# A decoder block in split fp32: the first projection stage with all sixteen k tiles split into high and low parts, and new orders behind it

## What is computed

```python
mod = silu_c @ w_ada[l] + b_ada[l]
sh1, sc1, g1, sh2, sc2, g2 = jnp.split(mod, 6, axis=-1)
h = modulate(rms_norm(x, norm1_w[l]), sh1, sc1)
proj = h @ w_in[l]
...
mixed = jnp.concatenate([y_ret, y_dif], axis=-1).astype(x.dtype) @ w_out[l]
x = x + g1[:, None, :] * mixed
h2 = modulate(rms_norm(x, norm2_w[l]), sh2, sc2)
mlp = jnp.square(jax.nn.relu(h2 @ w_mlp1[l])) @ w_mlp2[l]
x = x + g2[:, None, :] * mlp
return rms_norm(x, final_norm_w)
```

## Time and profile before

| | us |
|---|---|
| median of 3 runs | 2373.59 |
| lowest, highest | 2372.52, 2373.86 |
| profiled execution, its own time | 2372.57 |
| its span | 2370.7 |
| PE busy | 2312.1 (98%) |
| DVE busy | 1264.7 (53%) |
| ACT busy | 754.5 (32%) |

### The profile page before, as it was taken

One profiled execution on the slowest core, in us unless ns is written; L12 is line 12 of the kernel. 1 busy time (PEld: TensorE's weight loads), 2 busy tenths in 40 slices (PEclk: granted clock), 3 DMA queues, 4 the chain that ended last, 5 costly groups with the idle time before them and its releaser, 6 DMA issues.

```text
span 2370.7 us, 28575 instructions
## 1 busy us (share of the span) xinstructions
PE 2312.1 (98%) x10384; PEld 1883.6 (79%) x10384; DVE 1264.7 (53%) x1801; ACT 754.5 (32%) x1025; POOL 77.5 (3%) x59
## 2 busy tenths in 40 slices
PE   4999999999999999999999999999999999999998
PEld 2568888878787788888888888888888888888887
DVE  7977988866666675733333333333333333333354
ACT  3233343344545422421221221221221322222233
POOL 0011110100101000000000000000000000000000
PEclk9999999999999999999999999999999999999999
DMA  9956677622222574232222222222222222222222
GB/s 377 402 205 218 228 269 248 247 95 84 73 87 70 189 274 168 80 107 97 97 93 95 96 97 97 97 97 97 97 94 94 94 97 97 97 97 96 99 89 98
DMA packets 90630, 328.25 MB, mean 138 GB/s; under 512 B 10064, under 2 KB 10576, under 8 KB 89936
## 3 DMA queue, kind: packets, MB, share of 16 engines
q1 hardware_dynamic: 89568, 326.41, 39.3%
q10 hardware_dynamic: 1008, 1.13, 0.1%
HBM read 323.31 MB, written 4.19 MB: 138 GB/s over the span
## 4 chain that ended last, share of the span: by engine, by line
PE 87%; DVE 9%; ACT 2%; issue 1%; DMA 1%; POOL 0%; SPq 0%; POOLq 0%; ACTq 0%; DVEq 0%
PE bank L437 27%; PE bank L438 27%; PE bank L441 27%; DVE ada_sb L1058 3%; DVE w_lo L1051 2%; PE bank L578 1%; DVE prob L1058 1%; PE bank L544 1%; PE bank L461 1%; DMA xy<-x_t 1%; PE bank L569 0%; PE bank L492 0%; DMA prob<-ada 0%; ACT w_hi L757 0%; ACT L850 0%
## 5 line engine op out<-in xcount | busy, mean ns | idle before, releaser
L437 PE MATMUL bank<-act_hi,w_hi 128*128 128x512 f32 (+1 forms) x2112 | 828.8, 393 | 13.1 <-DVE act_lo L1098 4.6
L438 PE MATMUL bank<-act_lo,w_hi 128*128 128x512 f32 (+1 forms) x2112 | 819.9, 389 | 0.0
L757 ACT ACTIVATE w_hi<-raw 128x1024 fp32r<-128x1024 f32 x392 | 413.8, 1056 | 896.0 <-PE bank L441 841.5
L1051 DVE TENSOR_TENSOR w_lo<-raw,w_hi 128x1024 fp32r<-128x1024 f32 x392 | 491.9, 1257 | 308.9 <-ACT w_hi L757 296.0
L441 PE MATMUL bank<-act_hi,w_lo 128*128 128x512 f32 (+1 forms) x2112 | 518.3, 387 | 0.0
L437 PEld LDWEIGHTS bank<-act_hi,w_hi 128*128 128x128 f32 x2112 | 397.8, 188 | 101.5 <-issue 17.7
L438 PEld LDWEIGHTS bank<-act_lo,w_hi 128*128 128x128 f32 x2112 | 397.7, 188 | 81.9 <-issue 1.7
L441 PEld LDWEIGHTS bank<-act_hi,w_lo 128*128 128x128 f32 x2112 | 394.5, 188 | 81.1
L437 PE MATMUL bank<-u_hi,w_hi 128*128 128x512 f32 (+1 forms) x1040 | 401.6, 387 | 0.0
L438 PE MATMUL bank<-u_lo,w_hi 128*128 128x512 f32 (+1 forms) x1040 | 400.2, 386 | 0.0
L1453 DVE SCALAR_TENSOR_TENSOR xy<-bank,modr,xy 128x512 f32 (+1 forms) x141 | 105.9, 751 | 413.2 <-PE bank L441 413.2
(11 more groups left out here) (152 smaller groups left out, 1121.7 us busy)
## 6 DMA issues: line engine op xcount, KB each, us to landing
raw<-weights SPq DMA_DIRECT2D x400, 512.0 KB, 3.2
ada_sb<-ada SPq DMA_DIRECT2D x172, 512.0 KB, 5.4
prob<-ada SPq DMA_DIRECT2D x20, 512.0 KB, 6.7
xy<-x_t SPq DMA_DIRECT2D x16, 512.0 KB, 6.1
out<-rows_out SPq DMA_DIRECT2D x4, 1024.0 KB, 4.8
decay_sb<-decay SPq DMA_DIRECT2D x7, 256.0 KB, 3.1
silu_c<-c_row SPq DMA_DIRECT2D x1, 1024.0 KB, 5.6
rot_sb<-rot ACTq DMA_DIRECT2D x2, 256.0 KB, 7.1
```

Of the source, the lines that this page charges most:

```text
L437: pe.matmul(acc, stationary, hi, start=first, stop=False)
L438: pe.matmul(acc, stationary, lo, start=False, stop=False)
L757: nc.scalar.activation(w_hi[:, w], raw[:, r], ACT.Copy).then_inc(hi_ready, 1)
L1051: nc.vector.tensor_tensor(w_lo[:, w], raw[:, r], w_hi[:, w].bitcast(F32), ALU.subtract).then_inc(lo_ready, 1)
```

## The change

It changes eight things:

1. WHOLE is empty: all sixteen k tiles are split; a new `first_chunk` does all eight hi x hi products first, then hi x lo, then lo x hi, and the last tile's products bank by bank, with `first_done` telling when each bank is finished.
2. DVE's dot products take a row of 2048 in one instruction and start from the bias, so that two replace four, and `modulation1` becomes one small instruction (`scale1`). The rings have the same bytes: three places of 1 MB in the first stage (NADA_1 = 3), two later.
3. c comes as one row; PE spreads it over the partitions with a vector of ones, and ACT applies SiLU in four pieces between its squares. Three of the sixteen squares are summed by PE. The squares have places of their own in `rows_out`.
4. The stages of head 0 move one chunk later (`at = j - 1`), `rotate_q` of head 0 stands ahead of `rest_w`, and the rotary and decay tables are loaded behind the first stage's chunks.
5. Table loads of ACT are written out: one table set holds both Ln and Exp, and is loaded behind the gates.
6. In the output projection and the first MLP group one tile each goes to a spare bank (4 and 6), and two waits for a bank fall away; the last head's `finish_dif` and the splits of y stand earlier.
7. The sums for the second norm take the last tile's squares on PE instead of adding them on DVE first, and the sums and the spread stand inside the half tiles.
8. At the end `last_sums` stands ahead of the last turn, and rows are scaled and stored in halves of 512 KB.

```diff
-NADA = 4
-NADA_1 = 6
+NADA = 2
+NADA_1 = 3
...
-WHOLE = tuple(range(1, KT, 2))
+WHOLE = ()
...
             for k in range(KT):
-                for a in range(4 * k, 4 * k + 4):
-                    load_ada(Count(a))
-                    if a % 4 == 2:
-                        load_raw(Count(k))
+                if k == 0:
+                    for i in range(4):
+                        load_ada_half(i)
+                else:
+                    for e in range(2):
+                        load_ada(Count(2 * k + e))
+                load_raw(Count(k))
...
+                pe.wait_ge(hi_ready, made(Count(k)))
+                pe.wait_ge(act_hi_ready, k + 1)
+                for i in range(BLOCKS):
+                    product(i, w_hi, act_hi, start=k == 0)
+                pe.wait_ge(act_ready, SPLIT.index(k) + 1)
+                if k < KT - 1:
+                    for i in range(BLOCKS):
+                        product(i, w_hi, act_lo)
+                    pe.wait_ge(lo_ready, made(Count(k)))
+                    for i in range(BLOCKS):
+                        mm = product(i, w_lo, act_hi)
+                    mm.then_inc(chunk_done, 1)
+                else:
+                    pe.wait_ge(lo_ready, made(Count(k)))
+                    for i in range(BLOCKS):
+                        product(i, w_hi, act_lo)
+                        product(i, w_lo, act_hi, stop=True).then_inc(*((first_done, 1) if i < BLOCKS - 1 else (chunk_done, 1)))
...
             def project(h, s0, slots, stage):
+                head1 = isinstance(h, int) and h == 1
                 for j in range(slots):
-                    late = j == 0 and stage is ret_stage
-                    if j in stage and not late:
-                        stage[j](h - 1)
+                    at = j - 1 if head1 else j
+                    late = at == 0 and stage is ret_stage
+                    if at in stage and not late:
+                        stage[at](h - 1)
...
             round_w(Count(FIRST))
             round_rotated(1, q_hi)
             act.wait_ge(act_ready, KT)
-            for h in range(2):
-                take_gate(h, bank[3 + h], Count(FIRST))
+            for h in range(EARLY):
+                take_gate(h, bank[3 + h], first_done, 4 + h)
+            take_gate(EARLY, bank[3 + EARLY], chunk_done, FIRST)
             round_rotated(2, k_hi)
-            for h in range(2, EARLY + 1):
-                take_gate(h, bank[3 + h], Count(FIRST))
+            load_table(LN_EXP_SET)
...
+            for k in range(KT):
+                normed(0, k)
+                if k == 0:
+                    rest_w(Count(0))
+                    modulated_rest(0, 0)
+                if k + 1 < KT:
+                    dot1(k + 1, 0)
+                if k in SPLIT and k > 0:
+                    rest_w(Count(k))
+                    modulated_rest(0, k)
+                if k + 1 < KT:
+                    dot1(k + 1, 1)
+                    scale1(k + 1)
...
-            tile_part(Count(last), 7, 0, 1, chunk_done)
-            token_sums(2)
-            tile_part(Count(last + 1), 7, 1, 1, chunk_done)
-            token_spread(2)
+            tile_part(Count(last), 7, 0, 1, chunk_done, lambda: token_sums(2))
+            tile_part(Count(last + 1), 7, 1, 1, chunk_done, lambda: token_spread(2), BLOCKS // 2)
...
+            for part in range(2):
+                for half in range(2):
+                    cols = slice(half * HALF, (half + 1) * HALF)
+                    for tb, scaled in ((2 * part, scaled_v), (2 * part + 1, scaled_s)):
+                        sp.wait_ge(scaled, 2 * part + half + 1)
+                        sp.dma_start(out[tb * P128:(tb + 1) * P128, cols], rows_out[:, tb, cols]).then_inc(out_written, 16)
```

More of the change, by code:

```diff
@@ L52 @@
 FLOOR = -3.0e38
+SPARE_OUT, SPARE_UP = 4, 6
 LN_SCALE = 2.0 ** -64
+SILU_SET, LN_EXP_SET = 18, 6
 BLOCKS = 8
@@ L451, in first_chunk, with product @@
             def first_chunk(k):
[L453 to L454 removed]
+                w = w_place(Count(k))
+                def product(i, weight, moving, start=False, stop=False):
+                    return pe.matmul(bank[i][:], weight[:, w, i * P128:(i + 1) * P128], moving[:, k], start=start, stop=stop)
+                pe.wait_ge(hi_ready, made(Count(k)))
@@ L470, in quad_chunk, with tile_part, pairs, quad_part @@
                                 for i in range(BLOCKS)], s)
-            def tile_part(s, b, half, part, done):
+            def tile_part(s, b, half, part, done, between=None, at=BLOCKS):
                 cols = half_tokens(part)
-                split_products([(i, bank[b][:, cols], act_hi[:, 8 * half + i, cols], act_lo[:, 8 * half + i, cols],
-                                 half == 0 and i == 0, half == 1 and i == BLOCKS - 1, None)
-                                for i in range(BLOCKS)], s, done)
-            def quad_part(s, j, part, between, done):
+                def pairs(blocks):
+                    return [(i, bank[b][:, cols], act_hi[:, 8 * half + i, cols], act_lo[:, 8 * half + i, cols],
+                             half == 0 and i == 0, half == 1 and i == BLOCKS - 1, None) for i in blocks]
+                w = w_place(s)
+                pe.wait_ge(hi_ready, made(s))
+                for i, acc, hi, lo, first, _, _ in pairs(range(BLOCKS)):
+                    if i == at:
+                        between()
+                    stationary = w_hi[:, w, i * P128:(i + 1) * P128]
+                    pe.matmul(acc, stationary, hi, start=first, stop=False)
+                    pe.matmul(acc, stationary, lo, start=False, stop=False)
+                if between is not None and at == BLOCKS:
+                    between()
+                pe.wait_ge(lo_ready, made(s))
+                for i, acc, hi, _, _, last, _ in pairs(range(BLOCKS)):
+                    mm = pe.matmul(acc, w_lo[:, w, i * P128:(i + 1) * P128], hi, start=False, stop=last)
+                if done is not None:
+                    mm.then_inc(done, 1)
+            def quad_part(s, j, part, between, done, early=None):
                 cols, w = half_tokens(part), w_place(s)
```

425 lines of the change are left out of this document (239 added, 186 removed).

## The result

The changed kernel takes **2359.64 us** (median of four runs, 2359.62 to 2361.32) against 2373.06 for the kernel before (2372.16 to 2373.86): a ratio of 0.9946, 95% interval 0.993 to 0.9962. The forecast was 2360.5. The profiled execution is the slowest of the four: 2361.32 us, span 2359.4, which is 11.3 less than the span before.

The account below looks back on a forecast made before the run. It took DVE to set the first stage's pace and PE to bound the kernel behind it. Terms -2.8 - 8.7 - 1.2 = -12.7 us gave 2359.9 or 2360.9, forecast 2360.5, range 2354 to 2367.

Parts of the forecast that it names:

- Start: Chain up to the first `hf`: it begins at 25.8 us where it was at 29.81; bounds no gain or 5 us.
- Pace: First stage: DVE needs 7.1 us per k tile against 6.5, with a wide dot at 2.21.
- The slower DVE that eats PE's gain: First stage: DVE gets slower by 0.6 us a tile, and the 8 us that PE saves go into waiting.
- Behind the stage: From the stage's end through the first chunks: -5.0 + 2.6 - 0.4 = -2.8 us, with no change from the clock.
- the new wait: PE behind the first chunk after the stage waits 2.6 us for the second chunk's `w_hi`; bounds 0 to 3.5.
- The first rival: Behind the stage: no wait for `w_hi` or the clock stays, -17 us, 2356.5; chance 0.18.
- Later waits: PE's waits in heads, output projection, MLP and second norm shrink: -8.7 us, bounds -5 to -10.
- merged dots in the heads save DVE time beside PE: Heads, behind the first stage: wider dots save DVE time beside PE, counted as no change in total time.
- The second rival: PE's later waits only move: two thirds coming back gives -7 us, 2366.6, all gives -4, 2369.6; chance 0.12.
- End: Last rows scaled and stored in halves, sums ahead of the last turn: -1.2 us, bounds 0 and -2.
- Ring of three: First stage: three 1 MB places are too few, DVE waits 1.1 us in some 15 tiles, 2377; chance 0.06.
- clock in every tile: First stage: PE's wait of about 1.6 us a tile brings the lower clock, +50 us, 2411; chance 0.03.

Follow-up runs that it names:

- run 3: Changed kernel with the first stage's wide dots of tiles 1 to 15 starting from constant 0.0, not the bias: 2358.89 us.
- run 4: Changed kernel with seven odd k tiles (1 to 13) whole again, every other edit kept: 2358.46 us.
- run 1: Changed kernel with the second weight chunk's high part (`w_hi`) rounded ahead of `k_hi` and the table load: 2356.62 us.
- run 5: Changed kernel with seven whole k tiles and the second weight chunk's `w_hi` rounded right behind `q_hi`: 2352.41 us.
- run 9: Changed kernel with dots of 1024 behind the first stage, their sums in a free first-stage tensor so that no tensor moves: 2357.86 us.
- run 12: Changed kernel with seven whole k tiles, the early `w_hi` and dots of 1024 in the heads with no tensor moved: 2348.96 us.
- run 2: Changed kernel with only the Ln and Exp table load moved behind the second weight chunk's `w_hi`: 2357.57 us.
- run 7: Kernel before with only the table loads written out, one set for Ln and Exp loaded behind the gates: 2369.11 us.
- run 8: Changed kernel with dots of 1024 and a sum behind the first stage, which also moved later tensors by 64 bytes: 2365.18 us.
- run 10: Changed kernel with only 64 unused bytes in a partition ahead of the later tensors: 2366.81 us.
- run 11: Changed kernel with only 128 unused bytes in a partition ahead of the later tensors: 2379.36 us.

## Why the prediction was right

Its sum, -12.7, stands against -11.25 between the two profiled executions and -13.4 between the medians of the result. That 2360.5 is only 0.9 from the median is partly luck: the terms together were 1.4 too large, and the changed kernel's median lies 1.7 below its profiled execution, where the forecast put it 1.0 above.

- **Start**: -4.0 forecast, **-6.0** measured. Squares and SiLU were priced at 0.64 each from the earlier trace rows; eight squares in a row took 4.25, 0.53 each, so DVE's sum ended at 16.89, where 18.4 was forecast. The rest of the chain, forecast a little longer, became 0.2 shorter. POOL's root fell in it from 1.85 to 1.02, which the forecast had not named: before, a dot product ran on DVE beside it, and now DVE stands idle for it (1.20). No run changes the start alone, so this term is read from the traces.
- **Pace**: 7.1 us, measured **7.20**. The dot's price was the term: 2.21 taken, 2.27 measured. All of it is the start value that comes from a tensor: without it (run 3) the dot of 102.25 has the next instruction 2.21 behind it, as forecast, and a tile takes 7.08. Over fifteen tiles the 0.1 costs 1.5. The mask and lambda cost 0.4, forecast 1.0. With the start's 2.0 that puts the last `hf` at 132.21, where the sum gives 133.3; from it to the rotation it took 4.25, forecast 3.9. Misses of opposite sign made 136.46 for 136.9, not good numbers.
- **The slower DVE that eats PE's gain**: right. The waits for `act_lo` (1.13 a tile, forecast 1.4) and 9.93 of 10 us of DVE show it, and run 4 shows the other side: with seven whole tiles the stage ends six us earlier (four to five between runs 1 and 5 and runs 9 and 12). PE was busy 6.04 us in a tile, not the 5.44 of a later chunk, so instead of two waits of 1.6 together it has one of 1.13 in most tiles; only four times does it wait for `act_hi`. The forecast said that DVE gets slower, but did not draw the conclusion that splitting fewer tiles would do more for the stage.
- **Behind the stage**: bank 0 at 136.46 (136.9), `k_hi` at 144.51 (144.8), the new wait 2.53 (2.6), the clock loss 1.7 (1.7); -3.15 at the end of head 1 against -2.8. Runs 1 and 2 show that ACT's order is the cause of the wait. The first rival (0.18) is what run 1 builds: 2356.62, where it was priced at 2356.5.
- **Later waits**: -8.7 forecast, **-7.4** measured (from -3.15 at the end of head 1 to -10.6 at the last products). What was named went: `w_hi` and L544 by the table loads (run 7: 3.0 alone, where 2.4 was claimed, 1.0 of it from y's splits), y's splits, `xy`, `issue`; the second norm gave 2.4 of its 2.7, more than the 1.7 claimed. Only the table loads were isolated by a run; for the others the lists of waits before and after are the evidence. From 150 us on PE waits 4.4 us, where 2 to 4 was forecast. The step that failed is "merged dots in the heads save DVE time beside PE", at nothing: they hold POOL up, PE waits 1.7 for `sq_lo`, and by run 9 they cost 2.5 in the heads. The second rival, waits that only move, was thus true for about a fifth of this term, by a mechanism that it did not have. A last 0.9 for `sq` stands at the end (L837).
- **End**: -1.2 forecast, about **-0.7** (span -11.3 less PE's -10.6). The scaling starts 11.1 earlier, so 0.5 of it is the order ahead of the scaling and 0.2 the halved stores, which were to give 1.05. The dip is gone as forecast (DMA share 1.01 to 1.04 in every us from 2350 to 2358), but the stores run at 401 to 414 GB/s there, where those of 1 MB ran at 434 to 442 behind their dip (2366 to 2369). No run tells whether the size of the pieces is the cause.
- **Ring of three, clock in every tile**: neither came. DVE waits for no piece in the stage, at 362 GB/s, and the clock is 1.00 with a wait of 1.1 us in each tile. The Trainium skill's rule on idle gaps (TensorE: Matmul & The Clock Gate, Why this matters for your kernels), weighed in the prediction, remains in conflict: 2.5 us was followed by the lower level here, and in runs 3 and 8 to 11 also.

## What to carry to other kernels

When a stage is made to end earlier, read the next engine's whole list behind it: here one order on ACT cost 3.0 us by the medians with all tiles split (run 1), and 6.0 with seven whole tiles (run 5 against run 4), where it took back half of what the stage had gained. Ask of a part that makes the limiting engine slower what it buys elsewhere: splitting all tiles left the stage at 112.64 us. Merging instructions of an engine with slack is not free if another engine takes turns with it: look for an operation on the other engine whose duration has grown, and for what waits for it. After any edit that adds or removes a small tensor, compare the time of one unchanged chunk of the main loop before believing a difference of a few us.

## What was not expected of the hardware

- Where the moving operand lies in its partition changes the rate of a product in this kernel. A shift by 64 bytes made a chunk of 24 products 5.49 us, by 128 bytes 5.60, against 5.44; products on unmoved tensors kept theirs. The kernel before had 256 bytes more ahead of the same tensors than the changed one, and both have 5.44. Which alignment it is, and whether the read or the write of a neighbour is the cause, was not tried; the whole change could have been turned into a loss by it (2379.36).
- A dot product that starts from a value in a tensor takes 2.34 us at 2048 columns, one that starts from a constant 2.29 (the rows at 104.08 and, in run 3, at 102.25).
- TensorE's lower level (0.50) followed the waits of 2.4 and 2.5 us, and none of the waits of 1.1; it came during the wait of 5.3.
